# Norms in two GpSimd operations, x of the last stages in pairs of blocks, and other places for gates, first level and head results of linear attention

## The chip, the cores and the metric

The kernel runs on one core of a Trainium2 chip. The metric is the device time of one execution in microseconds (us), the median of several runs; lower is better. The engines are TensorE (PE in the rows, PEld for its weight loads), VectorE (DVE), ScalarE (ACT), GpSimd (POOL) and SyncE (SP), which issues the DMAs.

## The reference, cut to what matters

Eight stages work one after the other on h, 256 tokens by 1024 features, in float32. Stages 0, 2, 3, 5 are SwiGLU blocks with a norm before and after, stage 1 is a mixer of attention and convolution, stage 4 is gated linear attention, stage 6 is a second block's mixer and stage 7 its SwiGLU. The last two have an affine map on the normed x (scale and shift by feature).

```python
def rms_norm(x, g):
    y = x * lax.rsqrt(jnp.mean(x * x, axis=-1, keepdims=True) + NORM_EPS)
    return y * g
...
    h = h + FFN_RES * rms_norm(f, g[1])          # f: the block's output
...
def odd_mixer(h, w_in, w_gate, b_gate, norm_g, w_out):       # stage 4
    q, k, v, r, g_lr = jnp.split(h @ w_in, [...], axis=-1)
    g = jax.nn.log_sigmoid(g_lr @ w_gate + b_gate) / GATE_TAU
    o = gla_chunked(qh, kh, vh, gh)              # 4 heads, S_t = exp(g_t) S_(t-1) + k_t^T v_t, o_t = q_t S_t
    o = merge_heads(rms_norm(o, norm_g))         # norm by head, 256 columns
    return (o * jax.nn.silu(r)) @ w_out
...
    h = _rmsnorm(x, norm1_w) * (1.0 + scale1) + shift1       # stage 6; stage 7 alike
```

## The kernel before

**Products.** Every large matmul is made of three products of rounded parts (fp32r): high part of x by high part of w, high by low, low by high (L570, L571, L573). For that ScalarE rounds each weight tile (`whi`, L459) and VectorE subtracts (`wlo`, L468). The weights come in units of up to four blocks of 128 rows, cut into sub-units of two blocks; `raw` has 3 unit buffers, `whi` and `wlo` have 7 sub-unit buffers each, and `ahead` (L323) lets ScalarE and VectorE split five sub-units beyond the one that TensorE is at. The tokens are two halves of 128 (`tok` 0 and 1); a sub-unit is multiplied with both.

**Banks.** Of eight PSUM banks six (`acc`) take accumulations and two (`tb`) take transposes and small products; both are rings (L44), and a bank is used again when the signal that its last reader raises is there.

**Order.** Each engine has one program, written out by hand; an instruction that waits holds all behind it on its engine. `pe_chunk` (L619) runs a chunk of four sub-units and calls `at(i)` ahead of sub-unit i; `pe_down` (L636) runs a projection to h, with token half 0 ahead of half 1 by `lag` sub-units, `late` ahead of sub-unit 3 and `then` near its end, where the next stage's transposes of half 0 stand.

**Norms.** ScalarE squares 512 columns at a time and sums them (L682, `ss`, two columns). GpSimd adds the two sums (L696), scales and adds epsilon (L689) and raises to the power -0.5 (L691). `pool_rstd` does this for f, the output of a stage, and for h. In stages 6 and 7 ScalarE then multiplies h by the norm (`act_hn`, L1662), TensorE transposes that (L742), VectorE (L1692) and ScalarE (L1679) apply the affine map to four blocks each, ScalarE rounds them (L774) and VectorE subtracts (L769), in two halves of four blocks (512 columns). `pe_first` waits for a half ahead of sub-units 0 and 2.

**Stage 4.** Seven chunks (`GJ`): k, half of q with the gates' low-rank input, the other half of q, two of v, two of r. In chunk 2 TensorE makes the gates' dots (L1511, two `tb` banks); ScalarE takes Abs (L1578), Exp (L1582) and Ln (L1584) pair of heads by pair, VectorE takes min (L1593) from the same banks and scans (L1600). From chunk 3 on, the steps of nine levels of the attention are laid between the sub-units by `gla_steps` (L1332), 16 slots for four chunks, one list for all engines: "k" and "q" transpose; (n, "a") is GpSimd's reference of level n, (n, "e") ScalarE's Exp, (n, "m") the products with k and q (L1403, L1405; L1440 on GpSimd for even levels), and (n, 0), (n, 1) the dots of a token half on TensorE (L1376) with VectorE's masked copy to `gS` (L1420). After chunk 6 TensorE makes eight head results (L1490, L1493; 256 columns, a bank each); ScalarE squares each, GpSimd makes its norm, VectorE multiplies by norm and gain (L1626) and by silu(r), which `evac` has put in `gr` (L1629); TensorE transposes the product (`operand`, L742), ScalarE rounds, VectorE subtracts, and the down projection follows.

## Time and profile before

| | us |
|---|---|
| time, median of 3 runs | 1455.39 (1454.96 to 1455.93) |
| the profiled execution, its own time | 1456.73 |
| its span | 1454.9 |
| ScalarE busy | 720.1 (49% of the span) |
| VectorE busy | 946.7 (65%) |
| GpSimd busy | 162.5 (11%) |
| granted TensorE clock, mean | 0.998 |

The span is what the profile shows from the first to the last instruction; the execution's own time has what lies around it. A row of a timeline gives the start, the duration, engine, line, what is written from what, the number of like instructions merged (x4), and in brackets how long the engine stood idle ahead of it and who ended that. Matmuls overlap: the distance of two starts is what one costs.

### The profile page before, as it was taken

The numbers are of one execution on the slowest core, as the hardware profiler recorded it, in microseconds if no ns is written. First come the engines' busy times: TensorE is split into PE (matmuls) and PEld (weight loads), VectorE is DVE, ScalarE is ACT, GpSimd is POOL, SyncE is SP. The second block draws the span as 40 slices with busy tenths as digits, with TensorE's granted clock in tenths as the row PEclk, the third lists the DMA queues.
The fourth block names the chain that finished last, engine by engine and source line by source line (L and its number), as shares of the span: only waits on it lengthen the run. The fifth ranks groups of instructions, "written<-read, shape, count | busy, mean of one in ns | idle before, by whom it ended". The sixth has DMA issues, their size and how long they took to land.

```text
span 1454.9 us, 17894 instructions
## 1 busy us (share of the span) xinstructions
PE 1425.2 (98%) x6715; PEld 1175.4 (81%) x6715; DVE 946.7 (65%) x1323; ACT 720.1 (49%) x1052; POOL 162.5 (11%) x260
## 2 busy tenths in 40 slices
PE   7999999999999999999999999999999999999997
PEld 5888888778888888888878888887877788788886
DVE  5666567687665686675776866755468566755543
ACT  5454355455544355444654545445555734544442
POOL 1900010001000010000162100001443110100000
PEclk9999999999999999999999999999999999999999
DMA  8686765236867768868543488774856445465551
GB/s 270 202 257 207 254 203 202 66 96 203 261 207 251 253 198 257 259 210 267 188 157 123 147 239 245 224 253 138 211 167 195 138 174 173 159 202 174 176 210 64
DMA packets 236342, 286.51 MB, mean 197 GB/s; under 512 B 37028, under 2 KB 160464, under 8 KB 236256
## 3 DMA queue, kind: packets, MB, share of 16 engines
q1 hardware_dynamic: 236000, 285.25, 61.7%
q8 instruction: 54, 0.88, 0.3%
q14 instruction: 32, 0.26, 0.1%
q10 hardware_dynamic: 256, 0.11, 0.0%
HBM read 281.13 MB, written 4.20 MB: 196 GB/s over the span
## 4 chain that ended last, share of the span: by engine, by line
PE 92%; ACT 3%; DVE 2%; issue 1%; POOL 0%; DMA 0%; ACTq 0%; DVEq 0%; POOLq 0%
PE ps L570 28%; PE ps L573 28%; PE ps L571 28%; PE ps L856 2%; PE ps L742 1%; PE ps L1092 1%; ACT whi L459 1%; PE ps L1376 1%; DVE wlo L468 1%; PE ps L1043 0%; PE ps L1016 0%; ACT junk L682 0%; PE ps L994 0%; PE ps L1862 0%; DMA fold<-in_norm_g_dram 0%
## 5 line engine op out<-in xcount | busy, mean ns | idle before, releaser
L468 DVE TENSOR_TENSOR wlo<-raw,whi 128x1024 fp32r<-128x1024 f32 (+2 forms) x474 | 563.1, 1222 | 249.9 <-ACT whi L459 249.3
L459 ACT ACTIVATE whi<-raw 128x1024 fp32r<-128x1024 f32 (+2 forms) x474 | 472.2, 1042 | 245.0 <-PE ps L573 95.2
L570 PE MATMUL ps<-whi,xh 128*128 128x512 f32 (+2 forms) x1440 | 568.3, 395 | 9.3 <-DVE wlo L468 6.8
L571 PE MATMUL ps<-wlo,xh 128*128 128x512 f32 (+2 forms) x1440 | 555.6, 386 | 0.0
L573 PE MATMUL ps<-whi,xl 128*128 128x512 f32 (+2 forms) x1440 | 548.7, 386 | 0.0
L570 PEld LDWEIGHTS ps<-whi,xh 128*128 128x128 f32 x1440 | 271.2, 188 | 68.0 <-DVE wlo L468 9.7
L573 PEld LDWEIGHTS ps<-whi,xl 128*128 128x128 f32 x1440 | 270.8, 188 | 55.6
L571 PEld LDWEIGHTS ps<-wlo,xh 128*128 128x128 f32 x1440 | 271.5, 189 | 50.9
L570 PE MATMUL ps<-whi,gh 128*128 128x512 f32 x440 | 172.6, 392 | 0.0
L571 PE MATMUL ps<-wlo,gh 128*128 128x512 f32 x440 | 171.3, 389 | 0.0
L573 PE MATMUL ps<-whi,gl 128*128 128x512 f32 x440 | 153.5, 389 | 0.0
L696 POOL TENSOR_TENSOR st<-st 128x1 f32<-128x1 f32 x30 | 8.2, 273 | 1103.6 <-ACT junk L682 1103.0
L837 ACT ACTIVATE hid<-ps,st 128x256 f32<-128x256 f32 x88 | 41.4, 470 | 117.4 <-PE ps L573 116.1
L573 PEld LDWEIGHTS ps<-whi,gl 128*128 128x128 f32 x440 | 82.6, 188 | 17.4
L571 PEld LDWEIGHTS ps<-wlo,gh 128*128 128x128 f32 x440 | 82.7, 188 | 16.8
L570 PEld LDWEIGHTS ps<-whi,gh 128*128 128x128 f32 x440 | 82.6, 188 | 16.7
L843 DVE SCALAR_TENSOR_TENSOR hid<-ps,st,hid 128x256 f32<-128x256 f32 x88 | 42.1, 479 | 58.2 <-ACT hid L837 58.1
L867 DVE TENSOR_TENSOR gl<-ps,gh 128x512 fp32r<-128x512 f32 x55 | 38.0, 691 | 64.4 <-ACT gh L862 64.4
L862 ACT ACTIVATE gh<-ps 128x512 fp32r<-128x512 f32 x55 | 32.9, 598 | 73.3 <-PE ps L856 73.3
L488 DVE SCALAR_TENSOR_TENSOR adaacc<-adat,scol,adaacc 128x512 f32<-128x512 f32 x84 | 62.9, 749 | 0.0
L774 ACT ACTIVATE xh<-xtmp 128x512 fp32r<-128x512 f32 x32 | 19.4, 634 | 34.5 <-DVE xtmp L763 34.4
L1225 DVE SCALAR_TENSOR_TENSOR Y<-cx,vcol,Y 128x256 f32<-128x256 f32 x85 | 34.9, 481 | 0.0
(239 smaller groups left out, 926.2 us busy)
## 6 DMA issues: line engine op xcount, KB each, us to landing
raw<-in_ffn_w_in_dram SPq DMA_DIRECT2D x174, 512.0 KB, 5.2
raw<-in_ffn_w_out_dram SPq DMA_DIRECT2D x40, 1024.0 KB, 6.0
raw<-in_w_in_dram SPq DMA_DIRECT2D x26, 1024.0 KB, 5.0
adat<-in_w_ada_dram SPq DMA_DIRECT2D x96, 256.0 KB, 3.0
raw<-in_w_ffn_gate_dram SPq DMA_DIRECT2D x22, 512.0 KB, 4.0
raw<-in_w_ffn_up_dram SPq DMA_DIRECT2D x22, 512.0 KB, 5.1
raw<-in_hyb_w_in_dram SPq DMA_DIRECT2D x10, 1024.0 KB, 5.4
raw<-in_gla_w_in_dram SPq DMA_DIRECT2D x10, 1024.0 KB, 5.6
```

Of the source, the lines that this page charges most:

```text
L459: e.activation(split_of(whi, j), raw_of(j), ACT.Copy).then_inc(*whi_made.up(j))
L468: e.tensor_tensor(split_of(wlo, j), raw_of(j), split_of(whi, j).bitcast(F32), ALU.subtract).then_inc(*wlo_made.up(j))
L488: e.scalar_tensor_tensor(adaacc[:, :], adat[n % 2][:, :], sc, adaacc[:, :], ALU.mult, ALU.add).then_inc(*ada_added.up(c, k))
L570: e.matmul(ps[:, 0:n], a, whi_of(j, k), start=first and k == 0, stop=False)
L571: last = e.matmul(ps[:, 0:n], a, wlo_of(j, k), start=False, stop=False)
L573: last = e.matmul(ps[:, 0:n], b, whi_of(j, k), start=False, stop=final and k == subs[j][2] - 1)
L837: e.activation(hb[:, tok * 512 + 256:tok * 512 + 512], acc.of(st, J0[st] + 4 * c, tok)[:, 0:256], ACT.Silu, scale=rstd(("h", st, tok)) if ...
L843: e.scalar_tensor_tensor(hb[:, tok * 512:tok * 512 + 256], acc.of(st, J0[st] + 4 * c, tok)[:, 256:512], rstd(("h", st, tok)) if st < 7 els ...
L856: last = e.transpose(ps[:, j * 256 + tok * P:j * 256 + (tok + 1) * P], hb[:, tok * 512 + j * P:tok * 512 + (j + 1) * P], ident)
L862: e.activation(gh[:, c * 512:(c + 1) * 512], tb.of("hid", st, c)[:, :], ACT.Copy).then_inc(*ghi_made.up(st, c))
L867: e.tensor_tensor(gl[:, c * 512:(c + 1) * 512], tb.of("hid", st, c)[:, :], gh[:, c * 512:(c + 1) * 512].bitcast(F32), ALU.subtract).then_i ...
L1225: e.scalar_tensor_tensor(y_of(b), cx_of(b, k), conv_w(b, k), y_of(b), ALU.mult, ALU.add).then_inc(*tap_made.up(b, k))
```

## The change

Four things are changed. The norms: `pool_rstd` has two operations; the factor (1/1024, or for f of a SwiGLU stage four times that, for the 0.5 of the residual) goes as a scale into ScalarE's Square, and one GpSimd tensor_scalar adds the two sums and epsilon, with the second sum as a column operand. The norms of heads had two operations and keep them, with the factor in the Square as well. The x of stages 6 and 7: rounded and subtracted in four pairs of blocks (256 columns), on ScalarE between the affines, and `pe_first` waits ahead of each of the first four sub-units there. The steps of stage 4: all four Abs of the gates ahead of the first Exp; (1, "m") one slot earlier. The heads' results: two heads share a bank; half 0's stand ahead of sub-unit 2 of chunk 6, half 1's ahead of sub-unit 3, with the transposes of the first two heads of half 0 behind them; the squares and the first rounding stand ahead of chunk 6's silu on ScalarE; the product with silu(r) is made for two heads at a time (512 columns); the transposes of the other two heads of half 0 stand ahead of the projection's sub-unit 1. Parts left out here are renamings and the helpers `pe_x_half`, `act_operand_half` and `dve_operand_half` (one half of what `pe_x`, `act_operand` and `dve_operand` did) and `f_factor`, the 0.5 or 1.0 of a stage.

```diff
-                new = (xhi_made.at(st, tok, k // 2), xlo_made.at(st, tok, k // 2)) if c == 0 and k % 2 == 0 else ()
+                new = ()
+                if c == 0 and (st >= 6 or k % 2 == 0):
+                    x = (st, tok, k if st >= 6 else k // 2)
+                    new = xhi_made.at(*x), xlo_made.at(*x)
                 pe_part(e, bank[c, tok], j0 + i, xh, xl, 2 * k, 8, tok, *new)
...
         def pool_rstd(e, key, factor=1.0):
-            ss, v = col(2, "ss", key), col(1, "v", key)
+
+            ss, wk, rk = col(2, "ss", key), col(1, "w", key), col(1, "r", key)
             e.wait_ge(*squares.at(key, 1))
-            e.tensor_tensor(v, ss[:, 0:1], ss[:, 1:2], ALU.add).then_inc(*rstd_step.up(key, 0))
-            e.wait_ge(*rstd_step.at(key, 0))
-            pool_power(e, v, 1, 1.0 / D, key, factor)
+            e.tensor_scalar(wk, ss[:, 0:1], ss[:, 1:2], EPS * factor ** -2, ALU.add, ALU.add
+                            ).then_inc(*rstd_step.up(key, 1))
+            e.wait_ge(*rstd_step.at(key, 1))
+            e.tensor_tensor(rk, wk, mhalf[:, 0:1], ALU.pow).then_inc(*rstd_made.up(key))
...
-        GLA = [(1, "m"), (4, "a"), (3, "e"), (2, "m")]
+        GLA = [(4, "a"), (3, "e"), (2, "m"), "-"]
...
-                return [["k", (1, "a")], [(2, "a")], ["q", (1, "e"), (3, "a")], [(0, 0), (0, 1), (2, "e")]][i]
-            return GLA[4 * (i - 4):4 * (i - 3)]
+                return [["k", (1, "a")], [(2, "a")], ["q", (1, "e"), (3, "a")], [(0, 0), (0, 1), (2, "e"), (1, "m")]][i]
+            return [s for s in GLA[4 * (i - 4):4 * (i - 3)] if s != "-"]
...
+            def operand(tok, q):
+                pe_x_half(e, "gla", tok, q, gr[:, tok * D:(tok + 1) * D], [gla_gated.at(tok, q)],
+                          (xlo_made, "gla", tok, q))
             for c in range(3, 7):
                 def at(i, c=c):
                     for s in gla_steps(4 * (c - 3) + i):
                         pe_gla_step(e, s)
+                    if c == 6 and i >= 2:
+                        for hp in range(2):
+                            pe_gla_out(e, i - 2, hp)
+                    if c == 6 and i == 3:
+                        operand(0, 0)
                 pe_chunk(e, 4, GJ[c], [(gla_in, c, tok) for tok in range(2)], at)
...
+            def second(i):
+                if i == 1:
+                    operand(0, 1)
+
+            def late():
+                for q in range(2):
+                    operand(1, q)
...
+        def pe_gla_out(e, tok, hp):
+
+            ps = acc.next(("out", tok, hp), (gla_gated, tok, hp))
+            for done in acc.freed:
+                e.wait_ge(*done)
+            if (tok, hp) == (0, 0):
+                e.wait_ge(*lv_put.at(7, 1))
+                e.wait_ge(*lv_put.at(8, 0))
+                e.wait_ge(*gla_in.at(4, 1))
+            for hd in (2 * hp, 2 * hp + 1):
+                z = ps[:, hd % 2 * 256:hd % 2 * 256 + 256]
+                t = e.matmul(z, gS[:, hd * 256 + tok * P:hd * 256 + (tok + 1) * P],
+                             gv[:, tok * D + hd * 256:tok * D + (hd + 1) * 256], start=hd % 2 == 0, stop=tok == 0,
+                             skip_group_check=True)
+                if tok:
+                    t = e.matmul(z, gOFF[:, hd * P:(hd + 1) * P], gv[:, hd * 256:(hd + 1) * 256],
+                                 start=False, stop=True, skip_group_check=True)
+            t.then_inc(*gla_dot.up(tok, hp))
...
                             act_gla_step(e, s)
+                    if c == 6 and i == 3:
+                        for n in range(8):
+                            tok, hd = divmod(n, 4)
+                            if hd % 2 == 0:
+                                e.wait_ge(*gla_dot.at(tok, hd // 2))
+                            act_squares(e, out_of(tok, hd), ("gla", tok, hd), 0, 256 ** -0.5)
+                            if n == 5:
+                                act_operand_half(e, "gla", 0, 0)
                 for tok in range(2):
                     evac(c, tok)
-            for n in range(8):
-                tok, hd = divmod(n, 4)
-                e.wait_ge(*gla_dot.at(tok, hd))
-                act_squares(e, acc.of("out", tok, hd)[:, 0:256], ("gla", tok, hd), 0)
-                if n == 6:
-                    act_operand(e, "gla", 0)
+            act_operand_half(e, "gla", 0, 1)
...
                                  ACT.Abs, bias=vector("bg", hd)).then_inc(*gate_abs.up(hd))
+            for hp in range(2):
                 x = slice(hp * 512, (hp + 1) * 512)
                 e.wait_ge(*gate_abs.at(2 * hp + 1))
...
             def normed(tok, hd):
-                o = slice(tok * D + hd * 256, tok * D + (hd + 1) * 256)
-                ps, key = acc.of("out", tok, hd), ("gla", tok, hd)
-                e.wait_ge(*rstd_made.at(key))
+                z, key = out_of(tok, hd), ("gla", tok, hd)
                 if tok == 0 and hd == 0:
                     e.wait_ge(*s_row[row_slot["gla"]].at("gla"))
-                    e.wait_ge(*gla_in.at(6, 1))
-                e.scalar_tensor_tensor(ps[:, 0:256], ps[:, 0:256], rstd(key), rows[row_slot["gla"]][:, 0:256],
-                                       ALU.mult, ALU.mult).then_inc(*gla_normed.up(tok, hd))
-                e.wait_ge(*gla_normed.at(tok, hd))
-                e.tensor_tensor(gr[:, o], ps[:, 0:256], gr[:, o], ALU.mult).then_inc(*gla_gated.up(tok, hd))
-            for n in range(8):
-                normed(*divmod(n, 4))
-                if n == 3:
-                    dve_operand(e, "gla", 0)
+                e.wait_ge(*rstd_made.at(("gla", tok, hd | 1)))
+                e.scalar_tensor_tensor(z, z, rstd(key), rows[row_slot["gla"]][:, 0:256], ALU.mult, ALU.mult
+                                       ).then_inc(*gla_normed.up(tok, hd))
+
+            def gated_out(tok, hp):
+                o = slice(tok * D + hp * 512, tok * D + (hp + 1) * 512)
+                e.wait_ge(*gla_in.at(5 + hp, tok))
+                e.wait_ge(*gla_normed.at(tok, 2 * hp + 1))
+                e.tensor_tensor(gr[:, o], acc.of("out", tok, hp)[:, :], gr[:, o], ALU.mult).then_inc(*gla_gated.up(tok, hp))
+            for hd in range(4):
+                normed(0, hd)
+                if hd == 1:
+                    gated_out(0, 0)
+            dve_operand_half(e, "gla", 0, 0)
+            for hd in range(4):
+                normed(1, hd)
+                if hd == 1:
+                    gated_out(1, 0)
+            gated_out(0, 1)
+            gated_out(1, 1)
+            dve_operand_half(e, "gla", 0, 1)
...
-            e.wait_ge(*xlo_made.at(*((st, 0, 1) if tok else (st - 1, 1, 1))))
-            for b in range(4, 8):
+            e.wait_ge(*xtmp_read(st, tok, 1))
+
+            def hi(g, ready):
+                e.wait_ge(*ready)
+                e.activation(x_pair(xh, g, tok), xtmp_pair(g), ACT.Copy).then_inc(*xhi_made.up(st, tok, g))
+
+            def affine(b):
                 e.activation(ada_part(1)[:, b - 4, :], of_4(tb.of("x", st, tok, 1))[:, b - 4, :], ACT.Identity,
                              scale=gain[:, b:b + 1], bias=modc[:, shift + b:shift + b + 1]
                              ).then_inc(*x_affine.up(st, tok, b))
-            act_xhi(e, st, tok, 0, ada_part(0), x_scaled.at(st, tok, 0, 3))
-            act_xhi(e, st, tok, 1, ada_part(1), x_affine.at(st, tok, 7))
+            affine(4)
+            hi(0, x_scaled.at(st, tok, 0, 1))
+            affine(5)
+            hi(1, x_scaled.at(st, tok, 0, 3))
+            affine(6)
+            hi(2, x_affine.at(st, tok, 5))
+            affine(7)
+            hi(3, x_affine.at(st, tok, 7))
+
+        def x_pair(z, g, tok):
+            return z[:, g * 512:(g + 1) * 512].rearrange("p (k n) -> p k n", k=2)[:, :, tok * P:(tok + 1) * P]
+
+        def xtmp_pair(g):
+            return xtmp[:, g * 256:(g + 1) * 256].rearrange("p (k n) -> p k n", k=2)
+
+        def xtmp_read(st, tok, q):
+
+            if tok:
+                return xlo_made.at(st, 0, 2 * q + 1)
+            return xlo_made.at(st - 1, 1, 2 * q + 1 if st == 7 else q)
...
-            for q in range(2):
-                dve_xlo(e, st, tok, q, ada_part(q))
+            for g in range(4):
+                e.wait_ge(*xhi_made.at(st, tok, g))
+                e.tensor_tensor(x_pair(xl, g, tok), xtmp_pair(g), x_pair(xh, g, tok).bitcast(F32), ALU.subtract
+                                ).then_inc(*xlo_made.up(st, tok, g))
```

## Rows read from the trace of the kernel before

**Rows 1.** The page, part 1: busy time of each engine, share of the span, instructions

```profile
PE 1425.2 (98%) x6715; PEld 1175.4 (81%) x6715; DVE 946.7 (65%) x1323; ACT 720.1 (49%) x1052; POOL 162.5 (11%) x260
```

**Rows 2.** TensorE's waits in the whole run: total us, times, longest us

```profile
PE ps L742 <- ACT hid L1666: 2.5, 3, 1.1
```

**Rows 3.** Timeline of TensorE in stage 4: start, us, instructions [idle before <-releaser]

```profile
727.63 0.66 PE L994 MATMUL ps<-cst,hid 128*128 128x128 f32 x4 [0.38 <-DVE gX L1593]
729.08 0.66 PE L994 MATMUL ps<-cst,hid 128*128 128x128 f32 x4 [0.80 <-DVE gX L1593]
...
747.80 2.02 PE L1376 MATMUL ps<-gX 128*128 128x128 f32 x16 [1.72 <-DVE gX L1405]
```

**Rows 4.** Timeline of ScalarE and VectorE at stage 4's gates

```profile
725.25 0.82 ACT L1578 ACTIVATE gX<-ps,vcol 128x256 f32<-128x256 f32 x2
...
726.70 0.87 DVE L1593 TENSOR_SCALAR gX<-ps,vcol 128x256 f32<-128x256 f32 x2
...
728.15 0.88 DVE L1593 TENSOR_SCALAR gX<-ps,vcol 128x256 f32<-128x256 f32 x2 [0.58 <-ACT gX L1578]
```

**Rows 5.** Timeline of VectorE before the first level

```profile
740.55 1.36 DVE L1420 COPY_PREDICATED gS<-glev,ps 128x512 f32<-128x512 uint32 x2
...
745.07 1.38 DVE L468 TENSOR_TENSOR wlo<-raw,whi 128x1024 fp32r<-128x1024 f32 x1 [3.15 <-ACT whi L459]
```

**Rows 6.** Timeline of TensorE at the heads' results

```profile
791.52 0.39 PE L570 MATMUL ps<-whi,xh 128*128 128x512 f32 x1
791.75 0.39 PE L571 MATMUL ps<-wlo,xh 128*128 128x512 f32 x1
...
792.20 2.32 PE L1490 MATMUL ps<-gv,gS 128*128 128x256 f32 x10
...
796.52 0.60 PE L742 MATMUL ps<-cst,gr 128*128 128x128 f32 x4
798.23 0.63 PE L742 MATMUL ps<-cst,gr 128*128 128x128 f32 x4 [1.11 <-DVE gr L1629]
```

**Rows 7.** Timeline of GpSimd and VectorE at the heads' norms

```profile
793.54 0.19 POOL L689 TENSOR_SCALAR st<-st 128x1 f32<-128x1 f32 x1 [20.89 <-ACT junk L682]
...
794.45 0.19 POOL L689 TENSOR_SCALAR st<-st 128x1 f32<-128x1 f32 x1
...
794.40 0.49 DVE L1626 SCALAR_TENSOR_TENSOR ps<-ps,st,row 128x256 f32<-128x256 f32 x1 [7.15 <-POOL st L691]
```

**Rows 8.** Timeline of ScalarE and TensorE at stage 6's opening

```profile
1007.66 1.51 ACT L1679 ACTIVATE xtmp<-ps,modc,st 128x128 f32<-128x128 f32 x4
1009.05 1.16 ACT L774 ACTIVATE xh<-xtmp 128x512 fp32r<-128x512 f32 x2
...
1017.74 1.24 PE L742 MATMUL ps<-cst,hid 128*128 128x128 f32 x8 [0.84 <-ACT hid L1666]
```

**Rows 9.** Timeline of TensorE, and of GpSimd at the end: waits behind norms

```profile
327.84 0.47 PE L570 MATMUL ps<-whi,xh 128*128 128x512 f32 x1 [0.23 <-ACT xh L774]
...
1255.35 1.24 PE L742 MATMUL ps<-cst,hid 128*128 128x128 f32 x8 [1.14 <-ACT hid L1666]
...
1267.41 1.24 PE L742 MATMUL ps<-cst,hid 128*128 128x128 f32 x8 [0.49 <-ACT hid L1666]
...
1449.92 0.19 POOL L696 TENSOR_TENSOR st<-st 128x1 f32<-128x1 f32 x1 [5.69 <-ACT junk L682]
```

**Rows 10.** Timeline of VectorE and GpSimd at stage 7's second norm

```profile
1262.62 3.48 DVE L468 TENSOR_TENSOR wlo<-raw,whi 128x1024 fp32r<-128x1024 f32 x3
...
1263.54 0.35 POOL L696 TENSOR_TENSOR st<-st 128x1 f32<-128x1 f32 x1 [9.08 <-ACT junk L682]
1263.97 1.05 POOL L689 TENSOR_SCALAR st<-st 128x1 f32<-128x1 f32 x1
1265.10 1.41 POOL L691 TENSOR_TENSOR st<-st,mhalf 128x1 f32<-128x1 f32 x1
```

**Rows 11.** Groups by line and form, GpSimd: the one operation with a column operand

```profile
L1296 POOL TENSOR_SCALAR diag<-cst,vcol 128x128 f32<-128x128 f32 x36 | 33.3, 944 | 8.8 <-DVE vcol L561 8.8
```

More of the change, by code:

```diff
@@ L681, in act_squares, with pool_power @@
                 e.wait_ge(*done)
-            e.activation(spare[:, 0:src.shape[1]], src, ACT.Square, accum_out=col(2, "ss", key)[:, i:i + 1]
-                         ).then_inc(*squares.up(key, i))
-        def pool_power(e, v, n, mult, key, factor=1.0):
+            e.activation(spare[:, 0:src.shape[1]], src, ACT.Square, scale=scale,
+                         accum_out=col(2, "ss", key)[:, i:i + 1]).then_inc(*squares.up(key, i))
+        def pool_power(e, v, n, mult, key):
             wk, rk = col(n, "w", key), col(n, "r", key)
-            f = factor ** -2
-            e.tensor_scalar(wk, v, mult * f, EPS * f, ALU.mult, ALU.add).then_inc(*rstd_step.up(key, 1))
+            e.tensor_scalar(wk, v, mult, EPS, ALU.mult, ALU.add).then_inc(*rstd_step.up(key, 1))
             e.wait_ge(*rstd_step.at(key, 1))
@@ L706, in act_h_squares, with f_factor @@
                     e.wait_ge(*done)
-                act_squares(e, h[:, tok * D + n * 512:tok * D + (n + 1) * 512], ("h", st, tok), n)
+                act_squares(e, h[:, tok * D + n * 512:tok * D + (n + 1) * 512], ("h", st, tok), n, D ** -0.5)
+        def f_factor(st):
+            return 0.5 if st in FFN else 1.0
         def act_f_squares(e, st, tok, j0, nk):
@@ L730, in dve_residual, with pe_x_half @@
                                        ALU.mult, ALU.add).then_inc(*h_made.up(st + 1, tok, n))
+        def pe_x_half(e, key, tok, q, src, ready, last):
+            ps = tb.next(("x", key, tok, q), last)
+            for done in tb.freed:
+                e.wait_ge(*done)
+            for done in ready:
+                e.wait_ge(*done)
+            for j in range(4):
+                t = e.transpose(ps[:, j * P:(j + 1) * P], src[:, (4 * q + j) * P:(4 * q + j + 1) * P], ident)
+            t.then_inc(*x_turned.up(key, tok, q))
         def pe_x(e, key, tok, src, ready, last):
             for q in range(2):
-                ps = tb.next(("x", key, tok, q), last(q))
-                for done in tb.freed:
-                    e.wait_ge(*done)
-                for done in ready(q):
-                    e.wait_ge(*done)
-                for j in range(4):
-                    t = e.transpose(ps[:, j * P:(j + 1) * P], src[:, (4 * q + j) * P:(4 * q + j + 1) * P], ident)
-                t.then_inc(*x_turned.up(key, tok, q))
+                pe_x_half(e, key, tok, q, src, ready(q), last(q))
         def pe_enter(e, st, tok):
@@ L823, in pool_open @@
                 for tok in range(2):
-                    pool_rstd(e, ("f", st - 1, tok), 0.5 if st - 1 in FFN else 1.0)
+                    pool_rstd(e, ("f", st - 1, tok), f_factor(st - 1))
             for tok in range(2):
@@ L1500, in pe_gla @@
                     if q % 4 == 0 else (),
-                    lambda tok, n: [(squares, ("f", 4, tok), n), (f_scaled, 4, tok, n)], late=lambda: operand(1),
+                    lambda tok, n: [(squares, ("f", 4, tok), n), (f_scaled, 4, tok, n)], second, late,
                     lag=LAG[4], then=entry(e, 5))
+        def pe_gla_out(e, tok, hp):
+            ps = acc.next(("out", tok, hp), (gla_gated, tok, hp))
+            for done in acc.freed:
+                e.wait_ge(*done)
+            if (tok, hp) == (0, 0):
[11 more added lines that the diff above has]
+            t.then_inc(*gla_dot.up(tok, hp))
         def pe_gate_dot(e, hp):
@@ L1561, in act_gla, with out_of, act_operand_half, dve_operand_half @@
                     act_operand(e, "gla", 1)
+        def out_of(tok, hd):
+            return acc.of("out", tok, hd // 2)[:, hd % 2 * 256:hd % 2 * 256 + 256]
+        def act_operand_half(e, key, tok, q):
+            act_xhi(e, key, tok, q, of_4(tb.of("x", key, tok, q)), x_turned.at(key, tok, q))
+        def dve_operand_half(e, key, tok, q):
+            dve_xlo(e, key, tok, q, of_4(tb.of("x", key, tok, q)))
         def act_operand(e, key, tok):
             for q in range(2):
-                act_xhi(e, key, tok, q, of_4(tb.of("x", key, tok, q)), x_turned.at(key, tok, q))
+                act_operand_half(e, key, tok, q)
         def dve_operand(e, key, tok):
             for q in range(2):
-                dve_xlo(e, key, tok, q, of_4(tb.of("x", key, tok, q)))
+                dve_operand_half(e, key, tok, q)
         def act_gates(e):
@@ L1689, in dve_ada_x @@
             e.wait_ge(*x_turned.at(st, tok, 0))
[L1690 removed]
+            e.wait_ge(*xtmp_read(st, tok, 0))
             for b in range(4):
@@ L1741, in pool_ada_open @@
                 if st == 6:
-                    pool_rstd(e, ("f", 5, tok), 0.5)
+                    pool_rstd(e, ("f", 5, tok), f_factor(5))
                 pool_rstd(e, ("h", st, tok))
```

28 lines of the change are left out of this document (3 added, 25 removed).

## The prediction

> **What bounds the kernel now.** I read the page first, then TensorE's waits, then the timelines around each wait. TensorE is busy for 1425.2 of 1454.9 us [rows 1]: the kernel is a chain of matmuls on one engine, and an edit is worth only what it takes from, or adds to, the moments when TensorE stands still. The three longest kinds that the change can reach are in the rows: the waits for x in stages 6 and 7 (2.5 us in three waits, [rows 2]), one of 1.72 us ahead of linear attention's first level and two (0.38 and 0.80 us) at the gates [rows 3], and one of 1.11 us at the heads' results [rows 6]. Behind each I ask what came last, and what is late next once it is gone. A matmul of 512 columns starts every 0.23 us (791.52, 791.75; 0.228 over many, [rows 6]), so a sub-unit (two blocks, three products) takes 1.37 us for one token half and 2.74 us for both.
>
> **The gates (stage 4).** The transposes of k need the two tb banks in which the gates' dots lie, and each bank is free when VectorE's min (L1593) has read it. Each min waits for the Abs of its own pair. The first pair's min starts at 726.70 and is not moved. The second pair's Abs stands behind Exp and Ln of the first, so its min starts at 728.15 after an idle of 0.58 us that an Abs ended [rows 4]. With all four Abs in front, at a pitch of 0.37 us (two take 0.82 us, each some 0.46), the last ends near 726.8, and the second min follows the first: 726.70 + 2 x 0.37 = 727.44. That is 0.71 us earlier than 728.15. TensorE's second transposes (729.08) move by the same, since they could start at 727.63 + 0.44 = 728.07. Exp and Ln of pair 0 come 0.74 us later, but ScalarE's sum of work is the same, and VectorE's scans, which run back to back behind the later Ln, end no later. The 0.38 us ahead of the first transposes stays. **-0.65 us** (bounds -0.5 and -0.8).
>
> **The first level, (1, "m").** TensorE waits 1.72 us for L1405 [rows 3], and the two VectorE products of level 1 start only at 746.37, behind a `wlo` split at 745.07 for which VectorE had idled 3.15 us [rows 5]. In the new order the products stand behind the mask copies that start at 740.55 and take 1.36 us, in just that idle time: they are ready by 743.3, and TensorE comes for them at 745.9. The split behind them waits for ScalarE anyway, so nothing is queued late. GpSimd runs its level references then and may be held up by them, but its next result is wanted one sub-unit later. With the switch of operation the whole 1.72 us goes: **-1.75 us** (-1.6 to -1.9).
>
> **The heads' results.** Now five of the twelve result matmuls take 2.16 us (792.20 to 794.36, [rows 6]), 0.43 us each, and TensorE then waits 1.11 us for the gated product. The chain behind is square (ScalarE), two GpSimd operations at a pitch of 0.91 us per head (793.54, 794.45, [rows 7]), two VectorE operations per head. The change puts the four matmuls of token half 0 ahead of sub-unit 2 of the last chunk, and the eight of half 1 and the first transposes of half 0 ahead of sub-unit 3. Take 0 as the end of sub-unit 1. TensorE: 4 x 0.43 = 1.7; sub-unit 2 to 4.5; 8 x 0.43 to 7.9; transposes to 8.4; sub-unit 3 to 11.2. The first gated half (two heads) is ready at 0.9 + 0.2 (matmul's tail) + 0.8 (two squares, at the pitch of the Abs) + 1.8 (two heads on GpSimd) + 1.7 (two products and the gate) = 5.1 at most; wanted at 7.9. So the 1.11 us go. What is late next? All of half 1 is queued on VectorE behind `dve_operand_half(0, 0)`, which waits for ScalarE's rounding, which waits for those transposes: rounded at 9.15, subtracted by 9.8. Then come two norms and a gate of half 1 to 11.4, two norms to 12.3, and `gated_out(0, 1)` to 13.0. TensorE reaches the second transposes of half 0 after the down projection's first sub-unit at 11.2 + 1.37 = 12.6. That is a new wait of 0.4 to 0.5 us; the units behind it have splits ready, and half 1's transposes come two sub-units later. The bank of the projection's first group needs silu of chunk 6, half 0, which stands behind all eight squares and the first rounding: 10.65, against 11.2. It holds, with 0.5 us to spare. Two more changes between transposes or small matmuls and the large ones cost some 0.1 us each. -1.24 + 0.45 + 0.2 = **-0.6 us** (0 to -1.3).
>
> **x of stages 6 and 7 in pairs of blocks.** ScalarE's four affines start every 0.348 us (1007.66 to 1009.05) and the two roundings of 512 columns take 1.04 us [rows 8]. The trace has no rounding of 256 columns from SBUF; the nearest row is an Abs of that width, pitch 0.37 us [rows 4], and from below half of 0.52 us. I take 0.32 to 0.34, so four cost 1.3 us for 1.04, and the last now waits about 0.1 us for the affine directly ahead of it: +0.37 us on ScalarE for each half. VectorE has four subtractions for two, and no late start. What does TensorE gain? Nothing that I can find: its first sub-units of x start without a wait in both stages. What does it lose? In stage 6 ScalarE goes straight on to the squares of f, half 1, then to splits, the new h, its squares and hn, which TensorE awaits for 0.84 us (1017.74, [rows 8]). That chain moves by the full 0.37 us. In stage 7 the chain behind half 0 runs over VectorE, where the earlier first pairs win back the idle ahead of the subtractions: near zero. **+0.37 us** (+0.2 to +0.6).
>
> **Norms in two GpSimd operations.** Each `pool_rstd` loses a tensor_tensor of 0.19 us and its hand-over, 0.28 us from start to start (the kind at 1449.92, [rows 9]). The first operation that remains gets a column as second operand. Nearest rows: the same kind with constants, 0.19 us [rows 7], and the only one with a column, 0.944 us for 128 elements [rows 11], of which one element is a small part. I take 0.19. Where the norm ends a wait of TensorE this counts: stage 2 (0.23 us, [rows 9]): -0.23. The tail of the program, all of it behind the last norm: -0.27. Stage 7, half 0: the 1.14 us wait ends 0.26 earlier. Stage 7, half 1: GpSimd's three operations take 0.35, 1.05 and 1.41 us instead of 0.19, 0.19 and 0.55, beside three `wlo` splits of VectorE at 1262.62 with a pitch of 1.14 us [rows 10]; each ends shortly after one split has ended. With two operations the power ends after the second split, near 1265.2 instead of 1266.51. TensorE waits for hn until 1267.41 [rows 9] and could have started at 1266.8, so this wait goes entirely (-0.6 us), and TensorE comes 0.2 us earlier on the whole because VectorE's chain does. Stage 7 together: -0.84 (to -0.3 if the power is held until the third split). **-1.34 us** for the three places.
>
> The Trainium skill (SBUF — State Buffer, section "SBUF: two separate sides") says that a DVE operation with two SBUF inputs and a GpSimd operation share a port pair under an exclusive lock, and that the loser blocks for the whole instruction. By that rule one removed operation is worth one split of VectorE here, and the trace agrees (1.05 us for an operation of 0.19). Without such a lock the half-1 norm would give only 0.27 us, and the sum would be 0.5 us smaller.
>
> **The sum.** -0.65 - 1.75 - 0.6 + 0.37 - 1.34 = -3.97 us on a span of 1454.9, or 1450.9. The profiled execution took 1456.73 us with what lies around the span; the median of the runs shown is 1455.39, so 1455.39 - 4.0 = 1451.4, and I write 1451.5 us, 0.27% faster. A measurement of this kernel tells 0.2% (2.9 us) from no change, so the forecast lies 1.0 us beyond that bound.
>
> **The rivals.**
> 1. *The heads win nothing.* If each hand-over of the new chain costs 0.1 us more than I have written, the second transposes wait 1 to 1.5 us, and silu's bank holds the projection up too: heads' term +0.4, total -3.0: 1452.4. For it: nine steps in order on three engines, and only 0.5 us to spare at the bank. Chance 0.16.
> 2. *The column operand is dear.* If the new first operation takes 0.93 us, each norm grows by 0.46 us: stage 2, tail and stage 7's two halves go from -1.34 to about +1.4, total -1.2: 1454.2. For it only the row of 128 elements. Chance 0.08.
> 3. *Norms under VectorE's port (slower).* In the new place the eight heads' norms run beside VectorE's own work. If each takes what the disturbed pair of stage 7 does (1.05 + 1.41 + gaps = 2.55 us for 0.91, [rows 7, 10]), the four of half 1 bring 6.6 us to the second transposes, and the first half 0.3 beyond its slack: total +2.9, 1458.3, and slower than before from 4.0 us of such stall on. Against it: VectorE's work there reads its results from PSUM, and beside such work GpSimd kept its 0.91 us [rows 7]. Chance 0.03.
> 4. *The pairs hide something.* If half of the stage-6 chain had slack, the term is +0.1 and the total -4.3: 1451.1; inside the forecast.
>
> **How the numbers follow.** The forecast (1450.2 to 1452.6) has 0.73, rival 1 0.16, rival 2 0.08, rival 3 0.03. The bounds of the terms add to -5.2 and -1.9, so the range is 1450.2 to 1453.5; it leaves out rivals 2 and 3 and the thin ends. Faster by over 0.2% means below 1452.5: nearly all of the forecast's share but some of its upper end, and half of rival 1: 0.71. Within 0.2%: 0.26. Slower: 0.03.
>
> **What would show it.** Right: no wait of TensorE ahead of L1376 near 746, the second wait at the gates under 0.2 us, a wait of 0.3 to 0.6 us at the second transposes of the gated product, hn of stage 6 awaited for 1.1 to 1.3 us, only two GpSimd operations per norm with 0.19 us for the first, and stage 7's second hn without a wait. Wrong: a wait for silu's bank at the down projection, a first norm operation over 0.3 us, or a wait ahead of x's sub-units that I saw none of.

## The result, and the profile after

| | us |
|---|---|
| time after, median of 22 runs | 1453.51 (1452.19 to 1455.33) |
| time before, median of 22 runs beside them | 1455.50 (1454.70 to 1456.70) |
| ratio | 0.9986, 95% interval 0.9979 to 0.9992 |
| the profiled execution after, its own time and its span | 1452.88, 1451.1 |

The change makes the kernel 2.0 us (0.14%) faster. That is under the 0.2% bound of the prediction, which had forecast 4.0 us less. The range of the prediction ended at 1453.5, so the time lies at its very edge, on the side of too little gain. The kernel after, in the page's first part:

```profile
PE 1424.5 (98%) x6715; PEld 1174.8 (81%) x6715; DVE 951.2 (66%) x1327; ACT 721.0 (50%) x1060; POOL 162.1 (11%) x230
```

TensorE does the same work (against [rows 1]: 6715 matmuls, 0.7 us less). VectorE is 4.5 us busier, though it has only four instructions more (1327 for 1323 in the page): that is the first hint at what went wrong. TensorE's waits after (engine, line, releaser: total us, times, longest us):

```profile
PE ps L748 <- ACT hid L1712: 2.3, 3, 1.0
...
PE ps L1386 <- DVE gS L1430: 1.7, 2, 1.5
PE ps L748 <- DVE gr L1667: 0.4, 1, 0.4
```

The 2.5 us of [rows 2] are 2.3: the norms' place hardly moved. Linear attention's waits, 4.0 us before at the four places of [rows 3] and [rows 6], are 0.4 at the gates, 0.4 at the heads, and 1.7 in two waits behind the first level. Now place by place, each against its rows of before, in timelines as in [rows 3 to 10] (start, us, instruction, [idle before <-releaser]).

**Gates.** ScalarE, VectorE and TensorE after:

```profile
724.08 1.55 ACT L1613 ACTIVATE gX<-ps,vcol 128x256 f32<-128x256 f32 x4
...
725.53 1.65 DVE L1629 TENSOR_SCALAR gX<-ps,vcol 128x256 f32<-128x256 f32 x4
...
726.46 1.44 PE L1004 MATMUL ps<-cst,hid 128*128 128x128 f32 x8 [0.38 <-DVE gX L1629]
```

Against [rows 3, 4]: four Abs and four mins in one row each, and the second wait of 0.80 us is gone, the eight transposes being one row.

**Level 1 and what comes after it.** TensorE, VectorE and GpSimd after:

```profile
744.08 1.95 PE L1386 MATMUL ps<-gX 128*128 128x128 f32 x16
...
748.93 2.05 PE L1386 MATMUL ps<-gX 128*128 128x128 f32 x16 [0.17 <-DVE gS L1430]
...
773.51 1.16 PE L1386 MATMUL ps<-gX 128*128 128x128 f32 x8 [1.50 <-DVE gS L1430]
```

```profile
740.06 1.51 DVE L1413 TENSOR_TENSOR gX<-gX,gKT 128x512 f32<-128x512 f32 x1
741.49 1.65 DVE L1415 TENSOR_TENSOR gX<-gX,gQT 128x512 f32<-128x512 f32 x1
743.23 2.40 DVE L468 TENSOR_TENSOR wlo<-raw,whi 128x1024 fp32r<-128x1024 f32 x1
745.55 0.68 DVE L1415 TENSOR_TENSOR gX<-gX,gQT 128x512 f32<-128x512 f32 x1
...
765.25 1.76 DVE L1415 TENSOR_TENSOR gX<-gX,gQT 128x512 f32<-128x512 f32 x1
766.94 2.31 DVE L468 TENSOR_TENSOR wlo<-raw,whi 128x1024 fp32r<-128x1024 f32 x1
...
771.61 1.21 DVE L468 TENSOR_TENSOR wlo<-raw,whi 128x1024 fp32r<-128x1024 f32 x1
```

```profile
762.98 2.07 POOL L1441 TENSOR_TENSOR gX<-gB 128x512 f32<-128x512 f32 x1 [4.70 <-PE ps L1386]
765.01 3.15 POOL L1450 TENSOR_TENSOR gX<-gX,gKT 128x512 f32<-128x512 f32 x2
```

The 1.72 us of [rows 3] are gone, but the kernel before had a wait of only 0.61 us ahead of level 7's dots, where there are 1.50 now (row of before, TensorE's timeline):

```profile
775.79 1.16 PE L1376 MATMUL ps<-gX 128*128 128x128 f32 x8 [0.61 <-DVE gS L1420]
```

The VectorE rows point at the cause: the same product takes 0.68 us alone (745.55) and 1.65 to 1.76 us beside GpSimd's work; a split 1.21 us alone (771.61) and 2.3 to 2.4 beside it.

**Heads.** TensorE after:

```profile
797.50 0.63 PE L748 MATMUL ps<-cst,gr 128*128 128x128 f32 x4 [0.36 <-DVE gr L1667]
```

The 1.11 us of [rows 6] have become 0.36, at the second transposes. In GpSimd's timeline the heads' norms keep the 0.19 us of [rows 7] for the first operation, and 0.55 us for the power.

**Stage 6's opening.** TensorE and ScalarE after, against [rows 8]:

```profile
1013.09 0.38 PE L570 MATMUL ps<-whi,xh 128*128 128x320 f32 x1 [0.33 <-ACT junk L685]
...
1014.98 1.24 PE L748 MATMUL ps<-cst,hid 128*128 128x128 f32 x8 [0.77 <-ACT hid L1712]
```

```profile
1004.65 0.46 ACT L1730 ACTIVATE xtmp<-ps,modc,st 128x128 f32<-128x128 f32 x1 [0.28 <-issue]
...
1007.43 0.58 ACT L685 ACTIVATE junk<-ps 128x512 f32<-128x512 f32 x1
```

One wait of 0.84 us has become two, 0.33 + 0.77 us. ScalarE's four affines and four roundings take 1004.65 to 1007.43.

**Norms.** TensorE, GpSimd and VectorE after, at stage 7 and at the end, against [rows 9, 10]; at stage 2 the wait of 0.23 us is gone (326.63):

```profile
1251.68 0.52 PE L748 MATMUL ps<-cst,hid 128*128 128x128 f32 x3 [1.03 <-ACT hid L1712]
...
1263.72 0.52 PE L748 MATMUL ps<-cst,hid 128*128 128x128 f32 x3 [0.52 <-ACT hid L1712]
```

```profile
1249.83 0.30 POOL L699 TENSOR_SCALAR st<-st 128x1 f32<-128x1 f32 x1 [63.76 <-ACT junk L685]
1250.22 0.56 POOL L702 TENSOR_TENSOR st<-st,mhalf 128x1 f32<-128x1 f32 x1
...
1259.86 1.49 POOL L699 TENSOR_SCALAR st<-st 128x1 f32<-128x1 f32 x1 [9.08 <-ACT junk L685]
1261.43 1.39 POOL L702 TENSOR_TENSOR st<-st,mhalf 128x1 f32<-128x1 f32 x1
...
1446.22 0.30 POOL L699 TENSOR_SCALAR st<-st 128x1 f32<-128x1 f32 x1 [5.85 <-ACT junk L685]
```

```profile
1258.92 3.49 DVE L468 TENSOR_TENSOR wlo<-raw,whi 128x1024 fp32r<-128x1024 f32 x3
```

The norm's new first operation takes 0.30 us alone, not 0.19, and 1.49 us beside VectorE's three splits, as much as the two operations of before together (0.35 and 1.05, from 1263.54 to 1265.02). The wait of 0.49 us is 0.52.

**The ledger.** The two spans differ by 3.86 us, the medians by 2.0. To see where, I take two TensorE instructions that both kernels have in the same place, and compare the time from one to the other. But for the start and stage 6's sixth chunk, a stretch that a version leaves alone comes out within 0.11 us of before in the traces of the experiments below, so a stretch tells far more than the time of a whole run. The last column is what the same stretch gave in them ("alone" is that part of the change alone in the kernel before; "the other four" are the variants of the kernel after).

| stretch (us in the trace of before) | after against before | the same in other traces |
|---|---|---|
| program start, to 24.36 | -1.05 | -0.38 to -1.30, whatever the version |
| stage 2's norm, 315.34 to 359.53 | -0.14 | -0.15 alone |
| gates, 723.42 to 734.38 | -0.67 | -0.67 to -0.69 in the other four |
| level 1 to the end of level 7's dots, 734.38 to 779.30 | -0.41 | -0.78 alone; -0.71 in three of the other four |
| heads' results, 779.30 to 831.88 | -0.77 | -0.78 alone; -0.75 to -0.82 in the other four |
| stage 6's opening, 997.24 to 1042.43 | +0.25 | +0.33 alone; +0.26 or +0.27 in three of the other four |
| stage 6, sixth chunk, 1042.43 to 1061.90 | -0.86 | -0.41 to +2.90, whatever the version |
| stage 7's norms, 1242.43 to 1279.84 | -0.15 | -0.13 alone |
| behind the last matmul | -0.14 | -0.14 alone |

The stretches between these add 0.08 us. Two of the rows are no work of the change. At the start, the first matmul, which waits for the first load, started 0.24 us earlier (4.85 for 5.09), and TensorE's matmuls went over from a pitch of 0.43 us to one of 0.23 some 2 us sooner. In stage 6 TensorE before waited at 1053.47 for ScalarE, which had waited for weights (ScalarE before, TensorE before):

```profile
1044.61 2.01 ACT L459 ACTIVATE whi<-raw 128x1024 fp32r<-128x1024 f32 x2 [6.71 <-DMA raw<-in_w_in_dram]
...
1053.47 0.44 PE L2237 MATMUL ps<-cst,ar 128*128 128x128 f32 x2 [0.66 <-ACT ar L1869]
```

After the change the same matmuls follow at 1049.89 without a wait. That wait is 0.66, 0, 1.26, 1.18, 0.77, 1.99, 2.03, 1.99, 1.56 and 0.26 us in the profiles of before, after and the eight experiments below in their order. In two of them, experiments 5 and 6, it costs more than itself. TensorE starts again behind the wait of 2.03 and 1.99 us, and 1.2 to 1.3 us later its granted clock goes from 1.00 to 0.5 and the pitch of its matmuls from 0.23 to 0.43 us, the 1.2 GHz level, for some eight large matmuls (TensorE in experiment 6; the next one starts at 1054.28):

```profile
1053.85 0.63 PE L570 MATMUL ps<-whi,xh 128*128 128x512 f32 x1
```

The stretch is 2.90 and 2.87 us longer than before there, 1.5 us more than the longer wait alone. In experiment 4's trace a wait of the same 1.99 us left the clock at 1.00. What is left for the change is -3.86 + 1.05 + 0.86, -1.95 us, which agrees with the medians' 2.0.

### The profile page after: what moved, and what is told of

It is laid out like the page before. It is cut to its first block, busy times and chain, and to the rows that moved or that the text cites. A ratio compares the mean times of both kernels' runs of the same rounds, so it can differ in the third digit from the quotient of the medians.

```text
span 1451.1 us, 17880 instructions
## 1 busy us (share of the span) xinstructions
PE 1424.5 (98%) x6715; PEld 1174.8 (81%) x6715; DVE 951.2 (66%) x1327; ACT 721.0 (50%) x1060; POOL 162.1 (11%) x230
## 4 chain that ended last, share of the span: by engine, by line
PE 93%; DVE 3%; ACT 2%; issue 1%; POOL 0%; DMA 0%; DVEq 0%; ACTq 0%; POOLq 0%
PE ps L570 28%; PE ps L573 28%; PE ps L571 28%; PE ps L866 2%; PE ps L748 1%; PE ps L1102 1%; DVE wlo L468 1%; ACT whi L459 1%; PE ps L1386 1%; PE ps L1053 0%; PE ps L1026 0%; PE ps L1004 0%; DVE xtmp L1761 0%; PE ps L1933 0%; DMA fold<-in_norm_g_dram 0%
## 5 line engine op out<-in xcount | busy, mean ns | idle before, releaser
L699 POOL TENSOR_SCALAR st<-st 128x1 f32<-128x1 f32 x30 | 14.5, 485 | 1109.4 <-ACT junk L685 1109.4
L1306 POOL TENSOR_SCALAR diag<-cst,vcol 128x128 f32<-128x128 f32 x36 | 33.3, 943 | 7.9 <-DVE vcol L561 7.9
```

What stands on the lines that cost most here:

```text
L1306: e.tensor_scalar(diag[:, i * P:(i + 1) * P], ident, conv_w(b, k), None, ALU.mult).then_inc(*diag_made.up(i))
```

## The experiments

My theory after seeing the two traces: VectorE's operations that read two SBUF operands and GpSimd's operations hold each other up for whole instructions, and this took back much of the level's gain and all that stage 7's second norm was to bring. Each expectation tells what this theory and its rivals give. The Trainium skill (SBUF — State Buffer, section "SBUF: two separate sides") states this rule. A pair of operations that the theory makes meet at 746 us shows it. GpSimd and VectorE in the kernel after, then the same two in experiment 6, which changes nothing near them:

```profile
746.10 1.04 POOL L1441 TENSOR_TENSOR gX<-gB 128x512 f32<-128x512 f32 x1 [1.56 <-PE ps L1386]
746.15 2.08 DVE L468 TENSOR_TENSOR wlo<-raw,whi 128x1024 fp32r<-128x1024 f32 x1
```

```profile
746.28 2.14 POOL L1440 TENSOR_TENSOR gX<-gB 128x512 f32<-128x512 f32 x1 [1.58 <-PE ps L1385]
746.31 1.21 DVE L468 TENSOR_TENSOR wlo<-raw,whi 128x1024 fp32r<-128x1024 f32 x1
```

Alone they take 1.04 and 1.21 us. Each time one of the two keeps its own duration and the other takes 0.87 or 1.10 us more, most of the duration of its neighbour. If the two shared a rate, both would have become longer. So the rule of the Trainium skill holds here: one engine works and the other waits for the whole instruction. Which one goes first differs between executions in which this code is the same: experiment 5's trace goes as the kernel after, those of experiments 3, 7 and 8 go as experiment 6.

The first four make one part of the change alone in the kernel before. Their runs lie beside 33 of the kernel before, median 1457.11 us (1455.14 to 1459.78): this chip's runs scatter more than those of the result.

**1. The norms alone.**

```
-            e.tensor_tensor(v, ss[:, 0:1], ss[:, 1:2], ALU.add)
...
-            pool_power(e, v, 1, 1.0 / D, key, factor)
+            e.tensor_scalar(wk, ss[:, 0:1], ss[:, 1:2], EPS * factor ** -2, ALU.add, ALU.add)
...
+            e.tensor_tensor(rk, wk, mhalf[:, 0:1], ALU.pow)
```

> Only the norms in two GpSimd operations. Theory L (the operation with a column operand takes 0.30 us, and beside VectorE's splits it blocks as long as the two operations that it replaces): the norm is 0.17 us shorter where undisturbed and not shorter at stage 7's second hn, whose wait of about 0.5 us stays; time -0.3 to -0.6 us against before. Rival P (my prediction's sizes): that wait goes, -1.3 us.

Median 1456.60 us, ratio 0.9997 (0.9988 to 1.0006). TensorE's rows at stage 7:

```profile
1255.36 1.24 PE L746 MATMUL ps<-cst,hid 128*128 128x128 f32 x8 [1.03 <-ACT hid L1670]
...
1267.43 1.24 PE L746 MATMUL ps<-cst,hid 128*128 128x128 f32 x8 [0.50 <-ACT hid L1670]
```

The first wait loses 0.11 us of its 1.14, the second nothing (0.49 to 0.50), with no other part of the change there. So the norms' term fails by itself, and not through something that the other parts do in stage 7. In the time, -0.3 to -0.6 us and -1.3 us can't be told apart by these runs.

**2. The pairs alone.**

```
-            act_xhi(e, st, tok, 0, ada_part(0), x_scaled.at(st, tok, 0, 3))
-            act_xhi(e, st, tok, 1, ada_part(1), x_affine.at(st, tok, 7))
+            affine(4)
+            hi(0, x_scaled.at(st, tok, 0, 1))
...
+            hi(3, x_affine.at(st, tok, 7))
```

> Only x of stages 6 and 7 in pairs of blocks. Theory: ScalarE's chain in stage 6 grows by 0.37 us and TensorE waits that much longer there, in stage 7 nothing changes: +0.3 to +0.5 us. Rival: earlier first pairs save a wait of TensorE that I did not see: 0 or less.

Median 1457.18 us, ratio 0.9998 (0.9989 to 1.0006). In the trace TensorE gets a wait that it did not have, the 0.84 us of [rows 8] stay (0.85), and stage 7's waits are 1.17 and 0.51 us, for 1.14 and 0.49:

```profile
1015.17 0.38 PE L570 MATMUL ps<-whi,xh 128*128 128x320 f32 x1 [0.36 <-ACT junk L685]
```

So the pairs cost some 0.36 us in stage 6 and nothing seen in stage 7; in the time it is too little to be measured.

**3. Level 1 alone.**

```
-        GLA = [(1, "m"), (4, "a"), (3, "e"), (2, "m")]
+        GLA = [(4, "a"), (3, "e"), (2, "m"), "-"]
...
-                return [..., [(0, 0), (0, 1), (2, "e")]][i]
+                return [..., [(0, 0), (0, 1), (2, "e"), (1, "m")]][i]
```

> Only the products of level 1 one slot earlier. Theory L: the 1.72 us wait ahead of level 1 goes, but VectorE's and GpSimd's operations of the later levels now run side by side and hold each other up, and TensorE waits about 1.5 us instead of 0.6 us in the third of the four chunks: net -0.5 to -0.9 us. Rival P: the later wait stays at 0.6 us, net -1.7 us; the 1.5 us in the changed kernel came from the gates or the heads.

Median 1456.65 us, ratio 0.9997 (0.9988 to 1.0006). The 1.72 us ahead of level 1 are gone, and ahead of level 7's dots stands:

```profile
773.68 1.16 PE L1376 MATMUL ps<-gX 128*128 128x128 f32 x8 [1.48 <-DVE gS L1420]
```

1.48 us for 0.61: half of the gain is given back 26 us later, by this edit alone; -0.78 us is left over the whole stretch. A gain of 1.75 us that stays whole is ruled out by the trace.

**4. The heads' results alone.**

```
+                    if c == 6 and i >= 2:
+                        for hp in range(2):
+                            pe_gla_out(e, i - 2, hp)
+                    if c == 6 and i == 3:
+                        operand(0, 0)
```

> Only the heads' results between the sub-units of the last chunk. Theory: the wait of 1.11 us at the transposes goes, one of 0.3 to 0.5 us comes at the second transposes of half 0: -0.6 to -0.8 us. Rival: silu's bank or the norms beside VectorE's work hold the projection: 0 or more.

Median 1456.64 us, ratio 0.9994 (0.9985 to 1.0002). TensorE's rows:

```profile
799.32 0.63 PE L747 MATMUL ps<-cst,gr 128*128 128x128 f32 x4 [0.36 <-DVE gr L1665]
...
1053.59 0.44 PE L2281 MATMUL ps<-cst,ar 128*128 128x128 f32 x2 [1.99 <-ACT ar L1913]
```

The first row is the one of the full change (0.36 us for 1.11). The second shows why a single trace can hide such a gain: 0.78 us won here, 1.3 us more than before lost where the weights of stage 6 land late in this execution.

By their times alone none of these four can be told from no change: each interval holds 1. What they show, they show in their traces. The gates' new order was not run alone.

The other four change the kernel after, beside 31 runs of the kernel before, median 1456.50 us (1455.08 to 1459.93). The kernel after itself was not run beside them.

**5. Two products moved from GpSimd to VectorE.** The k products of levels 6 and 8, to which the 3.15 us of GpSimd at 765.01 belong:

```
-                if n % 2:
+                if n % 2 or n in (6, 8):
...
-            if j == "m" and n % 2 == 0:
+            if j == "m" and n % 2 == 0 and n not in (6, 8):
```

> The changed kernel with the k products of levels 6 and 8 on VectorE instead of GpSimd: VectorE has two operations of some 0.68 us more. Theory L (GpSimd's operations hold VectorE's up in the third of the four chunks; there 1.1 and 1.1 us of VectorE's time are held up by these two): TensorE's wait ahead of the dots of level 7 falls from 1.50 to 0.5 to 1.0 us. Rival C (VectorE is simply full there): it grows to 2.5 us or more. Time against before: -2 to -3.5 by L, -1 by C.

Median 1452.00 us (1451.44 to 1455.28), ratio 0.9967 (0.9956 to 0.9978). TensorE's row at level 7 and VectorE's ahead of it:

```profile
770.25 3.11 PE L1386 MATMUL ps<-gX 128*128 128x128 f32 x24
```

```profile
765.51 0.68 DVE L1413 TENSOR_TENSOR gX<-gX,gKT 128x512 f32<-128x512 f32 x1
766.12 0.68 DVE L1415 TENSOR_TENSOR gX<-gX,gQT 128x512 f32<-128x512 f32 x1
766.72 1.21 DVE L468 TENSOR_TENSOR wlo<-raw,whi 128x1024 fp32r<-128x1024 f32 x1
```

VectorE got one more product here and yet is done earlier: product, product and split take 765.51 to 767.93, where product and split of the kernel after take 765.25 to 769.25. The wait of 1.50 us is gone, the dots being one row. This is what the theory of mutual blocking says; that VectorE simply has too much to do there is ruled out, since it has more now. The gain is larger than I expected: the wait was to fall to 0.5 to 1.0 us and is nil, even the 0.61 us of before, and the time was to fall by 2 to 3.5 us and fell by 4.5. From level 1 to the end of level 7's dots the trace has -1.97 us against before, where the kernel after has -0.41 and the other three -0.71. It is also the best version of the study: it beats the kernel before, and lies 1.2 to 2.5 us below the three versions run beside it, which all keep that wait.

**6. The norm's first operation with two column operands as a tensor_tensor.** Epsilon is left out of these norms, so that the form can be that of [rows 9].

```
-            e.tensor_scalar(wk, ss[:, 0:1], ss[:, 1:2], EPS * factor ** -2, ALU.add, ALU.add)
+            e.tensor_tensor(wk, ss[:, 0:1], ss[:, 1:2], ALU.add)
```

> The changed kernel with the first operation of a norm a tensor_tensor of the two sums, epsilon (1e-6) left out of these norms. Theory L (the column operand costs 0.11 us and a second turn at the port): undisturbed the operation takes 0.19 us, at stage 7's second norm it takes 0.35 instead of 1.49 us, the power ends one split earlier, and TensorE's wait for hn there, 0.52 us, goes. Rival: any operation of GpSimd that starts beside these splits is held until the second one ends, the wait stays within 0.1 us of 0.52.

Median 1453.24 us, ratio 0.9982 (0.9973 to 0.9992). GpSimd's rows at stage 7's second norm and at the end, then TensorE's:

```profile
1263.14 0.35 POOL L699 TENSOR_TENSOR st<-st 128x1 f32<-128x1 f32 x1 [9.06 <-ACT junk L685]
1263.57 1.41 POOL L701 TENSOR_TENSOR st<-st,mhalf 128x1 f32<-128x1 f32 x1
...
1448.83 0.19 POOL L699 TENSOR_TENSOR st<-st 128x1 f32<-128x1 f32 x1 [5.97 <-ACT junk L685]
```

```profile
1266.35 1.04 PE L747 MATMUL ps<-cst,hid 128*128 128x128 f32 x8
...
1269.55 0.50 PE L570 MATMUL ps<-whi,xh 128*128 128x512 f32 x1 [0.77 <-DVE wlo L468]
```

0.19 us alone and 0.35 us beside the splits, for 0.30 and 1.49: it is the form with a column as its scalar that is dear, not one operation as such. The wait at stage 7's second hn goes, as the prediction had it for a first operation of that price; 0.18 us of it come back at the next wait for a split (0.77 us, 0.59 in the kernel after). Over stage 7's stretch the trace has -1.01 us against before, for -0.15 after the change and -0.84 in the forecast; at stage 2 it has -0.31 and behind the last matmul -0.28.

**7. The full change without the pairs.** The edit of experiment 2 undone in the kernel after.

> The changed kernel with x of stages 6 and 7 rounded in two halves again. Theory: the waits of 0.33 us for f's squares and 0.77 us for hn in stage 6 become one of about 0.75 us, 0.3 to 0.45 us less in all; stage 7 the same within 0.1 us. Rival: the pairs carry part of the gain, and a wait appears ahead of x's first sub-units.

Median 1454.48 us, ratio 0.9986 (0.9977 to 0.9996). Stage 6's opening has the one wait of 0.77 us and not the 0.33 us ahead of it; stage 7's waits are the same (1.01 and 0.52). So the pairs cost 0.33 us here too, which these runs can't resolve in time.

**8. The load of the gate rows 14 units later.** My reading of the late weights in stage 6 was that they queue behind the broadcast of the gate rows.

```
-                if u == U0[6] + 10:
+                if u == U0[6] + 24:
```

> The changed kernel with the broadcast load of stage 6's gate row 14 weight units later in SyncE's queue. Theory W (this load, some 9 to 10 us from issue to landing, holds the weight unit behind it, and TensorE waits 0 to 2 us in the sixth chunk of stage 6, differently from run to run): ScalarE's wait of 6 us for weights near 1042 us falls below 1 us, TensorE's wait near 1050 us is nil, and the times scatter less, median 0.5 to 1.5 us below the changed kernel's. Rival: the load is as much in the way at its new place, or the scatter comes from elsewhere: same median and scatter.

Median 1454.09 us (1453.18 to 1457.39), ratio 0.9983 (0.9975 to 0.9992). ScalarE still waits for the weights near 1040 us, where I expected less than 1 us:

```profile
1040.31 2.01 ACT L459 ACTIVATE whi<-raw 128x1024 fp32r<-128x1024 f32 x2 [4.95 <-DMA raw<-in_w_in_dram]
```

In the other nine traces that wait is 4.05 to 7.44 us, so 4.95 is an ordinary one with that load out of the way, and TensorE's small wait of 0.26 us in this trace is no sign against it: the kernel after had none with the load in its old place. The time, forecast 0.5 to 1.5 us lower than without this edit, lies between those of experiments 6 and 7, with as much scatter. That reading is wrong, and why the weights keep TensorE waiting for 0 to 2 us there is left open.

## Why the prediction was half right

**Gates: right.** Forecast -0.65, found -0.67 to -0.69 in all five traces that have the new order; the 0.38 us stay and the 0.80 us go, as written.

**Level 1: the wrong step.** Forecast -1.75, found -0.41 in the trace after, -0.71 in three variants and -0.78 alone (1.72 us won, 0.87 us lost at level 7). The local steps held: the products came in time and the wait of 1.72 us went. What failed is the sentence that GpSimd "may be held up by them, but its next result is wanted one sub-unit later". It looks at one direction and at one result. VectorE is held up just as much: two products at 740.06 take 3.16 us for 1.36, two splits 4.5 us for 2.4. And GpSimd's references and products, which the new order brings beside other work of VectorE, disturb it again at 765, 26 us on. The group row of the q products says it in one number, 0.79 us each before and 1.15 after (VectorE's groups by line and form, x count, busy us, mean ns of one; before, then after):

```profile
L1405 DVE TENSOR_TENSOR gX<-gX,gQT 128x512 f32<-128x512 f32 x8 | 6.2, 790 | 0.0
```

```profile
L1415 DVE TENSOR_TENSOR gX<-gX,gQT 128x512 f32<-128x512 f32 x8 | 9.2, 1148 | 0.0
```

The wait of 0.61 us at 775.79 stood in the trace of before: level 7 was already late, so it had no slack to take a shift, and I had not looked there. The difference between -0.41 and -0.71 is the pair at 746 us shown above: in the trace after GpSimd goes first, VectorE's split and the mask copy behind it end later, and TensorE gets the new wait of 0.17 us at 748.93 and is 0.44 us later behind it; where VectorE goes first there is no such wait. Experiment 5 answers the other way round: with two products of GpSimd gone from level 7's neighbourhood, the stretch wins 1.97 us, more than the forecast.

**Heads: right in mechanism, size -0.77 for -0.6.** The new wait at the second transposes was forecast at 0.4 to 0.5 us and is 0.36; silu's bank holds nothing up. Rivals 1 and 3 fall: the heads' norms kept their 0.19 and 0.55 us. The working has two slips that did no harm: 0.9 + 0.2 + 0.8 + 1.8 + 1.7 is 5.4 and not 5.1, still well before 7.9, and the term starts from -1.24, where the rows have a wait of 1.11 us.

**Pairs: right.** Forecast +0.37, found +0.3 in three comparisons (+0.33 alone, and +0.31 between the variants with the pairs and the one without), from ScalarE's sequence. The cost shows as a new wait of 0.33 us and not as a longer wait for hn, which I had named as the sign. Rival 4 falls.

**Norms: mis-sized.** Forecast -1.34, found about -0.4 (-0.14 at stage 2, -0.15 in stage 7, -0.14 at the end). The first operation was taken at 0.19 us from the row with constants; it is 0.30 us, so a norm saves 0.15 us (1249.83 to 1250.78, 0.95 us, for 1253.35 to 1254.45, 1.10 us) and not 0.28. And at stage 7's second norm it takes as long as the two before it, so that the 0.6 us there do not come. Rival 2 named the operand as the danger and had its price at 0.93 us, three times too much for an operation alone and too little beside VectorE's splits. Experiment 6 shows that with a first operation of 0.19 us the step would have held: -0.31, -1.01 and -0.28 are -1.6 us for the forecast -1.34.

**The sum, and luck.** -0.67 - 0.41 - 0.77 + 0.25 - 0.43 is some -2.0 us, half of the forecast. Two terms failed in the same way, by blocking between VectorE and GpSimd, which I had as rival 3 for the heads alone. There it did not occur: VectorE's operations beside the heads' norms read PSUM, and the norms kept their times. That 1453.5 us still touches the range is luck. The level's term and the norms' term each came out beyond their own bounds, and the range was wider than its terms: the bounds as written (-0.5, -1.6, 0, +0.6, and -0.8 for the norms) add to -2.3 and not to the -1.9 of the text, which would have ended the range at 1453.1. The estimate without a lock is off too: 0.27 us for stage 7's second norm in place of 0.58 makes the sum 0.3 us smaller, not 0.5. The profile's -3.8 us would have confirmed the forecast for the wrong reasons: half of it is scatter of the start and of the weights in stage 6.

## What to carry to other kernels

When a step moves to where VectorE is idle, look at who else is busy at that moment: an elementwise product that reads SBUF twice took over twice its time beside GpSimd here, and both engines' later work has to be followed to the next wait of TensorE, also one that is small today. It can pay to give VectorE more work only to keep GpSimd away from it. And judge a gain of some microseconds by a ledger of stretches over several traces: here a stretch came out within some 0.1 us from trace to trace, while one place that no version touches moved by 3.8 us between executions.

## What the runs showed of the hardware

- A GpSimd tensor_scalar on 128x1 with a column as its scalar took 0.30 us, the same with constants or a tensor_tensor 0.19. Beside back-to-back splits of VectorE they took 1.49, 1.05 and 0.35 us. The longer ones end shortly after the end of a split; why the form with a column loses one more turn than a tensor_tensor, which reads as many columns, I did not test.
- VectorE beside GpSimd: product of 512 columns 0.68 us alone, 1.51 to 1.76 where it was held up; split of 1024 columns 1.21 alone, 1.86 to 2.40 where it was held up. The pair at 746 us (1.04 and 2.08 us in one trace, 2.14 and 1.21 in another) shows that the cost falls on one of the two for a whole instruction, as the Trainium skill's rule says (SBUF — State Buffer, the section above).
- TensorE's pitch for 512 columns was 0.43 us, that of the 1.2 GHz level, up to 14 us after the start in one execution and 16.6 in another, and 0.23 from then on, but for one relapse to 0.43 us and a granted clock of 0.5 behind a wait of some 2 us in two of the ten traces; a third with such a wait had none. For the start the profile's column of granted clock shows 1.00 in both executions, so there it is read from the pitch. The Trainium skill (TensorE: Matmul & The Clock Gate, Part 1) says that the number of slow matmuls at the start differs from run to run of one kernel; the ten profiles agree: the first wait behind it starts up to 1.3 us apart, of which the first load makes 0.24 us between before and after.
